# Last expert's result added on chip through a 0/1 product, final norm tile by tile, layer 0's scores over 128 rows, in a two-layer hybrid diffusion step

## What is computed

```
x  = x + g1 * mixer(rms_norm(x) * (1 + sc1) + sh1)
xm = rms_norm(x) * (1 + sc2) + sh2
x  = x + g2 * ec_moe(xm)            # 16 experts, 64 + 16 tokens each
...
return rms_norm(x, final_norm_w)

def ec_moe(x):
    gate, idx = top_k(softmax(x @ router_w).T, cap)
    ye = down(silu(gate_proj(x[idx])) * up(x[idx])) * gate
    return zeros.at[idx].add(ye)
def attend(q, k, v):
    return softmax(q @ k.T * scale) @ v
```

## Time and profile before

| | |
|---|---|
| runs of the kernel before | 1646.95, 1651.71, 1648.54 us; median 1648.54 us |
| profiled execution | 1652.23 us |
| its span (what the trace covers) | 1650.4 us |
| mean granted TensorE clock | 0.889 of full speed |
| busy share of the span | PE 84%, PEld 57%, DVE 60%, ACT 48%, POOL 26% |
| DMA | 341.64 MB, mean 207 GB/s |

### The profile page before, as it was taken

How to read it: one execution, slowest core, us unless ns; L and a number is a source line. 1 busy time by engine, 2 the same in 40 slices (tenths; PEclk the granted TensorE clock), 3 DMA queues, 4 the chain that set the end, 5 groups by cost and what they waited for, 6 DMA issues and landing times. The chain is left out here.

```text
span 1650.4 us, 17566 instructions
## 1 busy us (share of the span) xinstructions
PE 1381.3 (84%) x6621; PEld 948.0 (57%) x6621; DVE 985.0 (60%) x1303; ACT 800.0 (48%) x1127; POOL 434.6 (26%) x256
## 2 busy tenths in 40 slices
PE   3489998699979559999994899988879389999991
PEld 0356566655448436666662787755458256666660
DVE  0624633344455668888885433856554678888871
ACT  0422213333332257777774427654432277777762
POOL 0300102034310113345334003345400204434521
PEclk7699999656779779999997899999989589999996
DMA  8378750040042399999992212022041699999944
GB/s 347 141 295 336 303 197 11 1 191 1 1 160 85 151 352 367 377 376 387 376 351 53 76 55 55 4 105 87 1 193 77 242 340 370 386 380 370 386 142 156
DMA packets 64204, 341.64 MB, mean 207 GB/s; under 512 B 16780, under 2 KB 21496, under 8 KB 45688
## 3 DMA queue, kind: packets, MB, share of 16 engines
q1 hardware_dynamic: 57976, 319.55, 50.7%
q0 software_dynamic: 6144, 20.98, 5.5%
HBM read 316.26 MB, written 24.24 MB: 206 GB/s over the span
## 5 line engine op out<-in xcount | busy, mean ns | idle before, releaser
L1767 DVE TENSOR_TENSOR wlow<-wraw,proj_rounded 128x2048 fp32r<-128x2048 f32 x96 | 216.8, 2286 | 5.2 <-ACT proj_rounded L1713 5.2
L1618 POOL TENSOR_TENSOR modrow<-modrow,proj 80x1024 f32<-80x1024 f32 x30 | 132.9, 4432 | 309.5 <-ACT modrow L1739 309.5
L1650 PE MATMUL psum<-wlow,proj_rounded 128*80 128x512 f32 x512 | 202.2, 395 | 0.0
L1713 ACT ACTIVATE proj_rounded<-wraw 128x2048 fp32r<-128x2048 f32 x96 | 179.8, 1907 | 9.2 <-PEq L1315 9.2
L1649 PE MATMUL psum<-proj_rounded 128*80 128x512 f32 x376 | 151.3, 402 | 2.1 <-DVE proj_rounded L1772 2.1
L1248 POOL TENSOR_SCALAR ring<-ring,small 128x640 f32<-128x640 f32 x64 | 100.1, 1566 | 197.6 <-DVE small L1195 196.8
L1651 PE MATMUL psum<-proj_rounded 128*80 128x512 f32 x376 | 148.3, 394 | 0.0
L1221 ACT ACTIVATE ring<-psum,small 128x640 f32<-128x640 f32 (+1 forms) x80 | 56.8, 709 | 133.7 <-DVE small L1189 133.5
L1186 DVE TENSOR_REDUCE small<-psum 128x1 f32<-128x640 f32 (+1 forms) x80 | 57.2, 715 | 98.9 <-PE psum L1160 98.7
L1650 PE MATMUL psum<-wlow,small_rounded 128*80 128x512 f32 x256 | 100.8, 394 | 0.0
L1650 PEld LDWEIGHTS psum<-wlow,proj_rounded 128*80 128x80 f32 x512 | 76.6, 150 | 39.7 <-issue 1.1
(11 more groups left out here) (446 smaller groups left out, 3236.3 us busy)
## 6 DMA issues: line engine op xcount, KB each, us to landing
wraw<-in_exp_w_gate_dram SPq DMA_DIRECT2D x32, 2048.0 KB, 14.0
wraw<-in_exp_w_up_dram SPq DMA_DIRECT2D x32, 2048.0 KB, 12.8
wraw<-in_exp_w_down_dram SPq DMA_DIRECT2D x32, 2048.0 KB, 13.4
ring<-in_ada_w_dram SPq DMA_DIRECT2D x29, 1024.0 KB, 7.0
hold<-in_ada_w_dram SPq DMA_DIRECT2D x14, 1024.0 KB, 6.5
ring<-in_ev_w_in_dram SPq DMA_DIRECT2D x4, 2048.0 KB, 11.7
xr<-x_rows SPq DMA_DIRECT2D x15, 512.0 KB, 7.2
proj<-mod_rows SPq DMA_DIRECT2D x12, 512.0 KB, 5.4
```

The lines of the kernel that those rows point to most:

```text
L1618: pool.tensor_tensor(ye[0:CAP, :], ye[0:CAP, :], g2[0:CAP, :], ALU.mult).then_inc(s["ye"], 1)
L1650: pe.matmul(dst, xs[:, 0, k, :], wl, start=False, stop=False)
L1713: act.activation(high_of(m, h), raw_of(m, h), ACT.Copy).then_inc(s["high"], 1)
L1767: dve.tensor_tensor(low_of(m, h), raw_of(m, h), high_of(m, h), ALU.subtract).then_inc(s["low"], 1)
```

## The change

**Scores.** `kT` becomes two buffers, one for each key group, 128 partitions high: `kT[0]` holds group 0's keys in partitions 0 to 63 and zeros below, `kT[1]` (in place of the tile `roped`) zeros in 0 to 63 and group 1's keys below. A score product of layer 0 takes all 128 partitions of `qT` and of the head's `kT`. GpSimd writes the zeros, VectorE copies the halves out of PSUM one by one. The buffer of probabilities moves to ring slot 5.

**Last expert.** The result of expert 15 is kept in SBUF (`y_last`) and split into `y_high` and `y_low`. `pick_last` (80 by 640) is 1 where a token's number equals the expert's index, made by a comparison with the loaded row `token_ids`. `last_result` multiplies both parts by it in the next block, four matmuls for a tile of 128 tokens and 1024 columns, and VectorE adds the sum to the loaded tile ("sel" and "add"). SyncE issues the loads of x inside `experts`, after the last matrix and after the fifteenth scatter. In `odd_front` expert 15's scatter to DRAM is still issued, after the loads; in `final_norm` there is none.

**Order in layer 0 to 1.** `tensor_last` goes ahead of `down(15)`; ScalarE rounds cuts 1 and 0 instead of 0, 1 and 2; VectorE makes only cut 1's remainder there. The remainders of cuts 0 and 2, the rounded part of cut 2 and the softplus go into `odd_front`'s plan ("split", "soft"). The `clear_semaphores` between `experts(0)` and `odd_front` goes.

**Final norm.** Root and reciprocal are made tile by tile.

```
-        kT = R2(NT + P)
+        kT = [R2(NT + P), roped.rearrange("p a b -> p (a b)")[:, 0:NT + P]]
...
-                            dve.tensor_copy(kT[:, (t + 1) * P:(t + 2) * P], bank(b, P)).then_inc(s["g_dve"], 1)
+                            own(dve.tensor_copy(kT[0][0:64, (t + 1) * P:(t + 2) * P], psum[0:64, b, 0:P]))
+                            dve.tensor_copy(kT[1][64:P, (t + 1) * P:(t + 2) * P], psum[64:P, b, 0:P]).then_inc(s["g_dve"], 1)
...
+                    pool.wait_ge(s["roped"], TILES)
+                    pool.memset(kT[1][0:64, :], 0.0).then_inc(s["zero"], 1)
+                    pool.wait_ge(s["mm"], 4 * TILES)
+                    pool.memset(kT[0][64:P, :], 0.0).then_inc(s["zero"], 1)
                     pool.wait_ge(s["late"], 16 * 11)
+                    pool.wait_ge(s["zero"], 4)
...
+        def last_result(pe, t, b):
+            for h in range(2):
+                part = slice(h * 512, (h + 1) * 512)
+                pe.matmul(bank(b + h), pick_last[0:CAP, t * P:(t + 1) * P], y_high[0:CAP, part], start=True, stop=False)
+                mm = pe.matmul(bank(b + h), pick_last[0:CAP, t * P:(t + 1) * P], y_low[0:CAP, part], start=False, stop=True)
+            return mm
...
+                    sp.wait_ge(s["mm"], M - 2)
+                    sp.dma_start(ids[0:CAP, :], A["token_ids"].to_broadcast([CAP, NT])).then_inc(s["ids"], 16)
+                    sp.wait_ge(s["mm"], M)
+                    sp.wait_ge(s["sc"], 16 * (NE - 1))
+                    for t in range(TILES):
+                        sp.dma_start(xr[:, t, :], x_rows[t * P:(t + 1) * P, :]).then_inc(x_in[t], 16)
...
-                    scatter(NE - 1)
-                    pool.wait_ge(s["sc"], 16 * NE)
+                    pool.wait_ge(s["sc"], 16 * (NE - 1))
...
-                    down(NE - 1)
                     if following:
                         following["tensor_last"](pe)
+                    down(NE - 1)
...
+                    for c in range(2):
+                        part = slice(c * 512, (c + 1) * 512)
+                        act.wait_ge(s["last"], c + 1)
+                        act.activation(y_high[0:CAP, part], y_last[0:CAP, part], ACT.Copy).then_inc(s["lasthigh"], 1)
...
+                    dve.tensor_scalar(pick_last[0:CAP, :], ids[0:CAP, :], idf[0:CAP, :], None, ALU.is_equal)
...
-                    dve.wait_ge(s["sc"], 16 * (NE - 1))
...
+                        dve.tensor_tensor(y_low[0:CAP, part], y_last[0:CAP, part], y_high[0:CAP, part], ALU.subtract)
...
+            plan = [("sel", 0), ("sel", 1), ("sel", 2), ("add", 0), ("add", 1), ("xs", 0), ("turn", 0), ("add", 2), ("xs", 1), ("sel", 3), ("apply", 0),
+                    ("turn", 1), ("unit", 0), ("add", 3), ("xs", 2), ("apply", 1), ("sel", 4), ("turn", 2), ("unit", 1), ("add", 4), ("xs", 3), ("apply", 2),
+                    ("evict", 0), ("turn", 3), ("unit", 2), ("xs", 4), ("apply", 3), ("evict", 1), ("turn", 4), ("unit", 3), ("split", 0), ("apply", 4), ("evict", 2),
+                    ("split", 2), ("soft", 0)]
...
                     def root(t):
-                        act.wait_ge(x_in[t], 16)
+                        act.wait_ge(s["add"], t + 1)
...
+                    for t in range(TILES):
+                        pool.wait_ge(x_in[t], 16)
+                    pool.indirect_dma_start(x_rows, bass.IndirectOffsetOnAxis(ap=idx[:, NE - 1:NE], axis=0), y_last[0:CAP, :], None, compute_op=ALU.add).then_inc(s["sc"], 16)
...
-                    act.activation(rstd, ssq, ACT.Sqrt, scale=1.0 / D, bias=EPS).then_inc(s["root"], 1)
+                        act.activation(rstd[:, t:t + 1], ssq[:, t:t + 1], ACT.Sqrt, scale=1.0 / D, bias=EPS).then_inc(s["root"], 1)
...
+                    add(0)
+                    add(1)
                     for t in range(TILES):
+                        dve.wait_ge(s["root"], t + 1)
+                        dve.reciprocal(rstd[:, t:t + 1], rstd[:, t:t + 1]).then_inc(s["recip"], 1)
...
                         dve.scalar_tensor_tensor(out=xr[:, t, :], in0=xr[:, t, :], scalar=rstd[:, t:t + 1], in1=nw, op0=ALU.mult, op1=ALU.mult).then_inc(s["y"], 1)
+                        if t + 2 < TILES:
+                            add(t + 2)
...
         def even_keys(h, t):
-            q = slice(64 * (h // 4), 64 * (h // 4) + 64)
-            return kT[q, 0:NT] if t < ST else kT[q, NT:NT + P]
+            k = kT[h // 4]
+            return k[:, 0:NT] if t < ST else k[:, NT:NT + P]
...
-        experts(0, ready, odd_ahead())
-        clear_semaphores()
-        odd_front()
+        experts(0, ready, odd_ahead(), x_in)
+        odd_front(x_in)
```

More of the change, by code:

```diff
@@ L1860, in odd_ahead @@
         def odd_ahead():
-            s = {n: sem("n1a_" + n) for n in ("rows", "turnrows", "par", "ab", "q", "own", "aown", "whigh", "w0", "w1", "w2")}
+            s = {n: sem("n1a_" + n) for n in ("rows", "turnrows", "par", "own", "whigh", "w0", "w1", "w2")}
             def sync_first(sp):
@@ L2134, in _ @@
                     for what, n in plan:
-                        if what == "turn":
+                        if what == "sel":
+                            if n >= 3:
+                                pe.wait_ge(s["add"], (2, 4)[n - 3])
+                            last_result(pe, n, SEL_BANK[n]).then_inc(s["sel"], 1)
+                        elif what == "turn":
                             turn(n)
@@ L2217, in _ @@
                     for what, n in plan:
-                        if what == "split":
+                        if what == "split" and n >= 2:
                             weights_high(n)
+                        elif what == "soft":
+                            own.link(act.activation(e_, par[:, row_at["rg_lambda"]:row_at["rg_lambda"] + 8], ACT.Abs))
+                            act.activation(e_, e_, ACT.Exp, scale=-1.0).then_inc(s["ab"], 1)
                         elif what == "xs":
@@ L2357, in _ @@
                             weights_low(n)
+                        elif what == "soft":
+                            soft()
+                        elif what == "add":
+                            dve.wait_ge(x_in[n], 16)
+                            dve.wait_ge(s["sel"], n + 1)
+                            dve.tensor_tensor(xr[:, n, :], xr[:, n, :], psum[:, SEL_BANK[n]:SEL_BANK[n] + 2, :].rearrange("p a n -> p (a n)"), ALU.add).then_inc(s["add"], 1)
                         elif what == "xs":
@@ L2407, in _, with final_norm @@
                         pool.tensor_tensor(xT[:, 4 + f, :], xg[:, f, :], th[2 * f], ALU.mult).then_inc(s["sum"], 1)
-        def final_norm():
-            s = {n: sem("f_" + n) for n in ("w", "sq", "root", "own", "y", "out")}
-            s_x = [sem(f"f_x{t}") for t in range(TILES)]
+        def final_norm(x_in):
+            s = {n: sem("f_" + n) for n in ("w", "sel", "add", "sq", "root", "recip", "y", "out")}
             cs = Carve(projf)
@@ L2426, in _ @@
                     sp.wait_ge(s["out"], 16 * TILES)
+                @block.tensor
+                def _(pe):
+                    for t in range(TILES):
+                        if t == 4:
+                            pe.wait_ge(s["add"], 1)
+                        last_result(pe, t, SEL_BANK[t]).then_inc(s["sel"], 1)
                 @block.scalar
@@ L2487, in build @@
         out_and_route(1, early, ready)
-        experts(1, ready, None)
-        final_norm()
+        x_in = [sem(f"x2_in{t}") for t in range(TILES)]
+        experts(1, ready, None, x_in)
+        final_norm(x_in)
 def tables():
```

137 lines of the change are left out of this document (68 added, 69 removed).

## The result

The changed kernel takes 1597.57 us (median of runs from 1592.86 to 1604.35), the kernel before beside it 1648.33 us: a ratio of 0.9692 with a 95% interval from 0.9646 to 0.9739. The profiled execution took 1601.95 us, its span 1600.1 us at a mean granted clock of 0.918 (before 0.889). The forecast was 1594 us; for the profiled execution it was 1597.7.

The account below looks back on a forecast made before the run. No single engine: TensorE slow-clocked in layer 0's attention, idle between layers and at the end. 32 + 13.5 + 9 = 54.5 us off 1652.2 gives 1597.7 profiled, median 1594; range 1585 to 1616, own range 1586 to 1602.

Parts of the forecast that it names:

- Scores: Layer 0's attention: scores over 128 partitions raise the clock, 140 to 108 us, gain 32 us, bounds 0 and 35.
- The 3 us: Layer 0's attention: added to layer 1's 105 us because the stage is entered at the lower clock level.
- Rival A: Layer 0's attention: the clock gate ignores padded partitions, stage stays 140 us, total 1626 us; chance 0.14.
- Rival B: Clock rises but drops at each pause, or one boundary gives half; total gain 35 to 47 us, 1601 to 1614; chance 0.17.
- Rival C: Layer 0's scores: products are paid by partitions, so 128 cost twice 64, total 1691 us; chance 0.03.
- Front: Ahead of layer 0's attention: added key copies and zero memsets cost 0 us, upper bound 1.7.
- Layer 0 to 1: Between the layers: earlier loads of x and the last expert's product by matmul gain 13.5 us, bounds 9 and 16.
- Turn 0: First "turn" on TensorE after layer 0's experts: starts at 897.7 against 911.53, 13.8 us earlier.
- The loss after it: Between the layers, after turn 0: 1 us for sel 4 and 0.3 us more.
- The sixteenth scatter beside VectorE: Between the layers: it runs on GpSimd beside busy VectorE, where a scatter took 7.16 us; sigmoids need it only tens of units later.
- The end: Final norm: loads of x asked for earlier, VectorE becomes the bound; gain 9 us, bounds 6 and 11.
- The 3.3 us after the last scatter: End of the experts' block: unexplained time GpSimd may need after its last DMA before the next block starts.

Follow-up runs that it names:

- the two halves within one execution: The changed kernel with only heads 4 to 7 of layer 0 over 128 partitions, heads 0 to 3 over 64: 1619.82 us in a single run.
- the repeat: The changed kernel, unchanged, measured again on another occasion: 1594.4 us against 1646.79 for the kernel before, ratio 0.9682.
- the first group: Kernels timed on one chip beside the kernel before (1651.64 us): the change's two halves, one half of the heads, and GpSimd's wait removed.
- its two repeats: The changed kernel, unchanged, measured again in two later groups: 1594.4 us and 1598.17 us.
- the one that came at 323.9: The changed kernel with layer 0's scores over 64 partitions again, all other edits kept: 1630.6 us, ratio 0.9889.
- the fills: The changed kernel with two unused matmuls in each wait ahead of an mLSTM unit: 1595.84 us against 1650.87 for the kernel before, ratio 0.9676.

## Why the prediction came out right

**Scores, 32 us predicted, 31.8 measured** (31.7 with this part alone). The step that took layer 1's stage as the measure and added 3 us for the entry gave 108, and 108.0 was measured. Shown: the attention's length follows the number of partitions of the score products (64: 139.8; 96 and 128: 54.0 us for the half), both between kernels and inside one execution. The stage took between 107.0 and 108.0 us in all ten profiled executions with 96 or 128 partitions, and 139.8 in both with 64.

The 3 us came out in their sum and not as worked out, which is in part luck. Counted from the first score, the seventh score product starts after 3.3 us where layer 1's, in the kernel before, starts after 1.7, and the last one after 90.6 against 89.0. So the entry at the lower level costs 1.6 us, about half of what I gave it. The other 1.6 us come behind the last score (17.4 us to the last value product against 15.8), where the clock is lower than in the stage that I measured by, 0.71 against 0.78. And the reading of the earlier trace rows passed over one thing: just before the clock fell at 398 us, PE was busy for only 0.72 of 2.00 us, so that row alone does not tell partitions from a pause. What does is the 10.00 of 10.00 us busy at 0.50 in the same rows, and the two halves within one execution.

**Rival A** (padding counts for nothing) is refuted by the 108.0 us of the scores alone. By data: ones and zeros in the keys give the same. By busy time: it has it the wrong way round. The Trainium skill, page "TensorE: Matmul & The Clock Gate", section "What's actually happening", has the gate set by how busy the PE has been. The runs disagree: PE busy 67.25 of 71.8 us went with 0.64, and 42.95 of 53.5 us with 0.90, in one stage of one execution.

**Rival B** has its first half in the traces: the clock does drop again, to a mean of 0.87 after 388 us. It did not cost what B put on it: the stage is 108.0 us long all the same. **Rival C** is refuted: 432 ns over 128 partitions against 429 over 64.

**Front, 0 predicted.** Confirmed: with the scores alone all the gain is the attention's.

**Layer 0 to 1, 13.5 predicted, 12.4 measured** (14.1 to the first unit, less the 1.7 after it). Turn 0 was to start 13.8 us earlier relative to the last product; it starts 864.41 - 853.63 = 10.78 us after it against 24.92, 14.1 earlier. The 1 us that I gave for a higher clock in turns 0 and 1 did not come: unit 0 follows turn 0 by 7.78 us, before by 7.79. The loss after it was put at 1.3 (sel 4 and 0.3) and was 1.7. The sixteenth scatter beside VectorE, put at 7.16 us and of no account, took 1.42 and was of no account.

**The end, 9 predicted, 7.1 to 9.0 measured** (end parts of 26.2, 24.3 and 25.7 us in three executions of the kernel after). VectorE is the bound as foreseen: from 1586.38 on it adds, inverts and scales without a gap of 0.1 us, and one add takes 1.22 us where I had 1.2. The chain up to the first root came out nearly as worked out (4.24 us to the first product against the 3.8 that I had, and 6.1 from there to the first reciprocal against 5.8). The term I left out is the wait for the weight of the final norm. Its load stood unchanged in the code, but I had moved the loads of x and the whole norm ahead, and what had been early became late: it is asked for when the block begins, takes 8.3 us behind the five loads of x, and holds the first scaling for 1.98 us. The experiment with the early load removes that wait in the trace, and its end part is 2.0 us shorter. The full 9.0 us of the repeat are luck in this respect: they hold the same wait, and make up for it by an earlier start of the block and a higher clock. The 3.3 us after the last scatter, which the prediction took from the trace without knowing what they are, are GpSimd's DRAIN of 2.6 us and what is around it.

**The sum.** 54.5 was predicted against the profiled execution, 50.3 came. The 4.2 us are the end (1.9), the boundary (1.1), and run-to-run movement of the stages that no edit touches, which gives 1.9 at the front and takes 2.3 in layer 1's attention; the 0.6 us on the rest and 0.2 for the scores close it. By medians the total is 3.6 us above the forecast, within the range of 1586 to 1602. One sum of the prediction does not come out: all upper bounds together, 62 us, lead from 1648.5 to 1586.5 us, so the lower end of 1585 lies below them and not 2 us short of them.

Open: why GpSimd's DRAIN takes 2.6 us once its last scatter has landed. What bounds the way from layer 0 to 1 there is narrow: GpSimd's DRAIN ends near 857.4, VectorE's near 857.5 and SyncE's at 857.2 us, so shortening one of them alone would win at most 0.1 us, an estimate from these three ends.

## What to carry to other kernels

Where two stages do the same work in different times, compare their granted clock before their engines: here it and PE's busy time, which follows it, were the only columns of work that differed, and the remedy was to let the scores contract over more partitions, which costs nothing in the product (432 ns for 128 partitions, 429 for 64). When a chain is moved forward, list every load that used to be early on it, also those whose lines the diff does not touch; the one left out became the next wait. Before you take a wait away, look up which engine ends the block next: here the next one was 0.3 us ahead of it. Gains of 2 us on such a kernel are visible in the trace and not in the time, so read them there and don't promise them.

## What the runs showed of the hardware

TensorE's mean granted clock was 0.66 in a stage of 64-partition scores although PE was busy over 90% of it (129.4 of 140 us), and half of the padding (96 partitions, 32 of them zeros) was enough to lift it to 0.91.

GpSimd's DRAIN at the end of the experts' blocks took 2.59 us in the kernel after, where it began once the scatter had landed, and 6.5 and 6.6 us where it began while one was under way.

The spread between executions of one kernel, 15 us for the kernel before in the first group (1640.60 to 1655.95), has a place in part. In thirteen traces the first score of layer 0 comes between 323.9 and 336.3 us. Of these 12.4 us, 3.9 arise ahead of the mLSTM stage (its first VectorE instruction comes at 261.71 and 265.59 us in the two), and 8.5 from there on. The mLSTM stage's clock is 0.66 or 0.67 in the profiled executions of the kernel before, of the kernel after and of its two repeats, and 0.93 to 1.00 in the one that came at 323.9. That spread over the first scores is not all clock: with 0.67 in all of them, the kernel after and its repeats still lie between 331.1 and 335.8. Windows of the first repeat of the kernel after:

```profile
285.00:295.00 10.00, 8.08 (x50) 7.43 (x50) 3.18 (x11) 3.67 (x13) 0.00 (x0) 0.67 0.00 0
295.00:305.00 10.00, 8.03 (x50) 7.40 (x50) 3.23 (x11) 3.56 (x14) 0.00 (x0) 0.66 0.00 0
```

The number of partitions is not the whole rule. My expectation for the fills said that this stage multiplies over 64 partitions; PE's work in it, in the kernel before from 285 to 315 us, is this:

```profile
L905 PE MATMUL psum<-proj,ring 128*128 128x129 f32 x48 | 11.4, 432 | 0.0
L897 PE MATMUL psum<-ring 64*128 64x129 f32 x48 | 6.3, 436 | 6.7 <-DVE proj L1035 6.7
L879 PE MATMUL psum<-ring_rounded 116*128 116x128 f32 x24 | 4.9, 344 | 0.0
```

Most of PE's time there goes to products over 128 and 116 partitions, with 6.7 us of waiting in 30, and the clock is at 0.66 all the same. So that 96 partitions or more hold the clock is shown for the scores of the attention, and not as a rule for the kernel. Layer 1's attention varies too, 104.8 to 108.8 us by how often its clock falls. What decides it in an execution, no run here shows.
